# First convolution chunk from half projections: ten taps ahead, small moves at the start of a hybrid encoder layer

## The reference

```python
h = rms_norm(x, norm_mix_g)
proj = h @ w_in                       # 1024 x 3840
a_val, a_gate, u, g_conv, g_ssm = split(proj)      # 768, 768, 256, 1024, 1024 columns
# convolution branch
v = a_val * sigmoid(a_gate)           # 256 x 768
v = causal depthwise convolution of v, 31 taps, + conv_b
v = silu(layer_norm(v)) @ w_conv_out
# state-space branch: 16 groups, 64 complex states each
bu = u @ B_bar;  scan x_t = A x_(t-1) + bu_t;  y = Re(C x) + d * u;  gelu; glu; @ w_ssm_out
m = sigmoid(g_conv) * y_conv + sigmoid(g_ssm) * y_ssm
x = x + m @ w_out
# then x += MoE(rms_norm(x)): 32 experts, top 4 of each token, 12 MiB of weights an expert
# and a final rms_norm
```

## Time and profile before

| | |
|---|---|
| median of 3 runs | 1145.58 us |
| profiled execution, its time / its span | 1142.67 / 1140.9 us |
| chain of work that ended last | PE 89%, DVE 9% |
| PE busy | 1113.5 us, 98% |
| DVE busy | 273.7 us, 24% |
| ACT busy | 179.5 us, 16% |
| POOL busy | 75.9 us, 7% |
| DMA, 431.62 MB on the queue of SP | 91.2% of 16 engines' span |

### The profile page before, as it was taken

The page is one execution under the profiler, slowest core; times in us unless marked ns, Lnnn a source line. Parts: engine busy times, 40 slices in busy tenths (PEclk is TensorE's granted clock), DMA queues, the critical chain, the costliest instruction groups (busy, mean ns, idle before and its releaser), DMA issues.

```text
span 1140.9 us, 12748 instructions
## 1 busy us (share of the span) xinstructions
PE 1113.5 (98%) x4959; PEld 490.8 (43%) x4960; DVE 273.7 (24%) x661; ACT 179.5 (16%) x333; POOL 75.9 (7%) x155
## 2 busy tenths in 40 slices
PE   7999899899999999999999999999999999999997
PEld 6888685533333333333333333333333333333332
DVE  3999761311111111111111111111111111111112
ACT  3011221111111111111111111111111111111112
POOL 2975100000000000000000000000000000000000
PEclk9999899799999999999999999999999999999999
DMA  8843479489999999999999999999999999999994
GB/s 225 268 157 139 159 304 374 185 327 410 418 418 428 430 427 429 429 427 430 427 429 429 429 429 429 427 430 427 428 429 427 430 427 428 429 429 429 429 427 191
DMA packets 51618, 431.89 MB, mean 379 GB/s; under 512 B 6465, under 2 KB 22255, under 8 KB 25390
## 3 DMA queue, kind: packets, MB, share of 16 engines
q1 hardware_dynamic: 51598, 431.62, 91.2%
HBM read 430.56 MB, written 1.05 MB: 378 GB/s over the span
## 4 chain that ended last, share of the span: by engine, by line
PE 89%; DVE 9%; issue 1%; ACT 1%; DMA 0%; DVEq 0%; another core or an unknown queue 0%; SPq 0%; POOL 0%; POOLq 0%
PE bank L1286 39%; PE bank L1298 20%; PE bank L1306 10%; DVE bank L814 6%; PE bank L1259 5%; PE bank L1265 3%; PE bank L1221 2%; PE bank L1186 2%; PE bank L1078 2%; PE bank L1278 1%; DVE bank L835 1%; PE bank L1270 1%; PE bank L1174 1%; PE bank L1252 1%; DVE ring L843 0%
## 5 line engine op out<-in xcount | busy, mean ns | idle before, releaser
L1286 PE MATMUL bank<-ring,area 128*64 128x512 f32 x2048 | 451.7, 593 | 0.8 <-DMA ring<-w_gate_up 0.8
L1286 PEld LDWEIGHTS bank<-ring,area 128*64 128x64 f32 x2048 | 147.4, 137 | 281.8 <-issue 273.5
L1298 PE MATMUL bank<-ring,area 128*64 128x512 f32 x1024 | 226.8, 595 | 1.0
L969 DVE TENSOR_SCALAR area<-bank 128x512 f32<-128x512 f32 x32 | 22.1, 692 | 769.8 <-PE bank L1286 769.8
L1298 PEld LDWEIGHTS bank<-ring,area 128*64 128x64 f32 x1024 | 70.7, 137 | 136.6 <-issue 127.9
L1306 PE MATMUL bank<-area,spT 128*128 128x512 f32 x256 | 118.4, 605 | 0.0
L1078 PE MATMUL bank<-area,ring 128*128 128x256 f32 x480 | 109.4, 388 | 1.2 <-DVE area L751 1.2
L1078 PEld LDWEIGHTS bank<-area,ring 128*128 128x128 f32 x480 | 92.5, 195 | 16.8 <-DMA ring<-w_in 1.4
L660 ACT ACTIVATE area<-area 128x512 f32<-128x512 f32 x32 | 20.2, 630 | 497.7 <-DVE area L969 497.7
L1306 PEld LDWEIGHTS bank<-area,spT 128*128 128x128 f32 x256 | 46.0, 189 | 71.9 <-issue 71.9
L814 DVE SCALAR_TENSOR_TENSOR bank<-ring,spread,bank 128x256 f32<-128x256 f32 x174 | 69.0, 481 | 0.0
(11 more groups left out here) (241 smaller groups left out, 522.8 us busy)
## 6 DMA issues: line engine op xcount, KB each, us to landing
ring<-w_gate_up SPq DMA_DIRECT2D x120, 2048.0 KB, 30.3
ring<-w_down SPq DMA_DIRECT2D x60, 2048.0 KB, 28.7
ring<-w_gate_up SPq DMA_DIRECT2D x16, 1024.0 KB, 12.0
ring<-w_in SPq DMA_DIRECT2D x15, 1024.0 KB, 9.6
ring<-w_down SPq DMA_DIRECT2D x8, 1024.0 KB, 13.2
ring<-w_out SPq DMA_DIRECT2D x1, 4096.0 KB, 14.0
ring<-w_conv_out SPq DMA_DIRECT2D x1, 3072.0 KB, 12.7
rows<-x SPq DMA_DIRECT2D x2, 512.0 KB, 3.8
```

Source lines behind the costliest of these rows:

```text
L969: return v.tensor_scalar(gc, bank[4][:, :], 7.0, None, ALU.min)
L1286: last = mm(bank[4 + b][64 * h:64 * h + 64, :], heT[:, k % 4, k // 4 * 64:k // 4 * 64 + 64], w[:, b * FF + h * 512:b * FF + h * 512 + 512] ...
L1298: last = mm(bank[6][64 * h:64 * h + 64, :], actT[:, k % 4, k // 4 * 64:k // 4 * 64 + 64], w[:, k % 2, h * 512:h * 512 + 512], start=(k == ...
```

## The change

It has these parts.

- PE makes the first halves (m = 0) of the first two chunks, `a_gate` and `a_val` of channels 0 to 127, first; then the transposes of the taps' weights; then the two second halves. The halves lie in four banks (`half_bank`). New semaphores `half_pe` and `half_sig`.
- ACT takes the sigmoid of each half by itself. The copy of the taps' weights moves behind the two Sin and the first half's sigmoid.
- DVE multiplies each half by itself (`gated_half`), and runs the taps of block 0 alone until `LEAD = 10` are done. From there even blocks (lane 0) and odd blocks (lane 1) take turns, lane 0 being ten taps ahead. In the scan loop 8 instructions follow each scan, the last too. The wait for `raw_ready`, which protects the memory that the finished block 0 is written to, moves to the last tap of block 0.
- SP issues the second chunk of `w_in` directly behind the first, ahead of the taps' weights, and `ssm_b` ahead of `ssm_c`.
- ACT runs one Sqrt on constants before it waits for x.
- POOL's block of ones is made once, in `pick`, where `ones_1` was made; the later `ones` and its count in the wait at L1147 go. The product for the rank waits for 7 instead of 8.

```diff
-SCAN_TAPS = 4
+SCAN_TAPS = 8
+LEAD = 10
...
+        half_bank = [[bank[5][:, 0:T], bank[4][:, 0:T]], [bank[6][:, 0:T], bank[3][:, 0:T]]]
...
             load_win(0)
+            load_win(1)
             sp.dma_start(tap_rows, conv_w[0]).then_inc(tap_in, 16)
+            for ri, src in enumerate((ssm_b_re, ssm_b_im)):
+                sp.dma_start(ssb[:, ri, :, :], src[0].rearrange("(t g) p h -> (g p) t h", g=2)).then_inc(ssm_in, 16)
             for ri, src in enumerate((ssm_c_re, ssm_c_im)):
                 sp.dma_start(cld[:, ri, :, :], src[0].rearrange("(c g) h p -> (g h) c p", c=2)).then_inc(c_in, 16)
-            for ri, src in enumerate((ssm_b_re, ssm_b_im)):
-                sp.dma_start(ssb[:, ri, :, :], src[0].rearrange("(t g) p h -> (g p) t h", g=2)).then_inc(ssm_in, 16)
-
-            load_win(1)
...
-            g.memset(ones_1, 1.0).then_inc(ones_ready, 1)
+            g.memset(ones, 1.0).then_inc(ones_ready, 1)
...
-            g.memset(ones, 1.0).then_inc(consts, 1)
...
+            act.wait_ge(consts, 1)
+            s.activation(neg_top, ident[:, 0:2], ACT.Sqrt)
             for t in range(TT):
                 act.wait_ge(x_in[t], 16)
...
-            act.wait_ge(params_pe, 2)
-            s.activation(taps[:, :, :], bank[7][:, 64:64 + KC * W].rearrange("p (k w) -> p k w", w=W), ACT.Copy)\
-                .then_inc(params_sb, 1)
...
             s.activation(pw[:, 0, 0, :], ra, ACT.Sin).then_inc(act_sin, 1)
+            act.wait_ge(half_pe, 1)
+            s.activation(sig_a[:, 0, :], half_bank[0][0], ACT.Sigmoid).then_inc(half_sig, 1)
+            act.wait_ge(params_pe, 2)
+            s.activation(taps[:, :, :], bank[7][:, 64:64 + KC * W].rearrange("p (k w) -> p k w", w=W), ACT.Copy)\
+                .then_inc(params_sb, 1)
+            act.wait_ge(win_pe, 1)
+            s.activation(sig_a[:, 1, :], half_bank[0][1], ACT.Sigmoid).then_inc(win_act, 1)
...
+            def gated_half(m):
+
+                if m == 0:
+                    dve.wait_ge(half_pe, 2)
+                    dve.wait_ge(half_sig, 1)
+                else:
+                    dve.wait_ge(win_pe, 2)
+                    dve.wait_ge(win_act, 1)
+                ins = v.tensor_tensor(vT[:, m, W - 1:PADT], sig_a[:, m, :], half_bank[1][m], ALU.mult)
...
+            lanes = [[(k, w) for k in range(half, KC, 2) for w in range(W)] for half in range(2)]
+            order = lanes[0][:LEAD]
+            for n in range(KC // 2 * W):
+                order += lanes[0][LEAD + n:LEAD + n + 1] + lanes[1][n:n + 1]
...
+                for k, w in some:
+                    if w == 0 and k in (1, 2, 4):
+                        if k == 1:
+                            gated_half(1)
                         else:
...
+                            gated(k // 2)
+                    if (k, w) == (0, W - 1):
+                        dve.wait_ge(raw_ready, 1)
+                    tap(k, w)
...
-            gated(0)
-            dve.wait_ge(raw_ready, 1)
+            gated_half(0)
             dve.wait_ge(params_sb, 2)
-            taps_of(0, range(W))
-            gated(1)
-            taps_of(1, range(W))
-            gated(2)
+            scanning = len(order) - SCAN_TAPS * ST
+            taps_of(order[:scanning])
...
-                taps_of(2, range(SCAN_TAPS * t, SCAN_TAPS * (t + 1) if t < ST - 1 else W))
+                taps_of(order[scanning + SCAN_TAPS * t:scanning + SCAN_TAPS * (t + 1)])
...
-            project(0)
+            project(0, (0,))
+            project(1, (0,))
             pe.wait_ge(tap_in, 16)
...
-            project(1)
+            project(0, (1,))
+            project(1, (1,))
...
-            pe.wait_ge(consts, 7)
             pe.wait_ge(conv_done, KC)
```

More of the change, by code:

```diff
@@ L126, in build @@
         bdown = ring[0:E, 20 * CH:20 * CH + D]
[L127 removed]
+        tri = at(20, 128, 1024)
         rows = sb("rows", [128, TT, D])
@@ L147, in build @@
         pick = sb("pick", [128, TT, CAP])
+        ones = pick[:, :, :].rearrange("p t s -> p (t s)")
         spread = sb("spread", [128, TT, 2, CAP])
@@ L230, in build @@
         win_dve = sem("win_dve")
+        half_pe = sem("half_pe")
+        half_sig = sem("half_sig")
         bu_pe = sem("bu_pe")
@@ new lines, in _, with tap @@
+            last_tap = {}
+            def tap(k, w):
+                src, acc = vT[:, k, w:w + T], bank[2][:, k % 2 * T:k % 2 * T + T]
+                if w == 0:
+                    if k >= 2:
+                        dve.wait_ge(conv_done, k - 1)
+                    ins = v.tensor_scalar(acc, src, taps[:, k, 0:1], p_cb[:, k:k + 1], ALU.mult, ALU.add)
+                else:
+                    dve.wait_ge(dve_own, last_tap[k])
+                    ins = v.scalar_tensor_tensor(conv[:, k, :] if w == W - 1 else acc, src, taps[:, k, w:w + 1], acc,
+                                                 ALU.mult, ALU.add)
+                if w == W - 1:
+                    ins.then_inc(conv_done, 1)
+                else:
+                    own[0] += 1
+                    last_tap[k] = own[0]
+                    ins.then_inc(dve_own, 1)
@@ L1054, in _ @@
                 pe.wait_ge(diag_ready, t + 1)
-                last = mm(bank[6][:, t * 128:t * 128 + 128], ones_1, diag[:, t, :], start=True, stop=True)
+                last = mm(bank[6][:, t * 128:t * 128 + 128], ones, diag[:, t, :], start=True, stop=True)
             last.then_inc(spread_pe, 1)
@@ L1077, in project @@
                             pe.wait_ge(hT_ready, k + 1)
-                        last = mm(win_bank(n)[:, m * T:m * T + T], w[:, k, m * 128:m * 128 + 128], hT[:, k, :],
-                                  start=(k == 0), stop=(k == KD - 1))
+                        last = mm(half_bank[n][m] if n < 2 else win_bank(n)[:, m * T:m * T + T],
+                                  w[:, k, m * 128:m * 128 + 128], hT[:, k, :], start=(k == 0), stop=(k == KD - 1))
                 if 1 in ms:
                     last.then_inc(win_pe, 1)
+                elif n < 2:
+                    last.then_inc(half_pe, 1)
             def raw_transpose(raw, b):
```

27 lines of the change are left out of this document (8 added, 19 removed).

## The result

The changed kernel takes 1135.32 us in the median of 9 runs (1133.2 to 1140.17), the kernel before in the same comparison 1144.92 us (9 runs, 1142.28 to 1146.0). The profiled execution took 1134.46 us with a span of 1132.7 us; before 1142.67 and 1140.9. So the profiled executions differ by 8.2 us where the forecast had 6.4, and the medians by 9.6.

The account below looks back on a forecast made before the run. PE bounds nearly throughout, except DVE's convolution taps from about 30 to 130 us; PE and DMA are at their limit in the experts. 3.7 us (DVE) + 2.7 us (clock) = 6.4 us, giving 1139.2 us, range 1137.0 to 1142.8 us.

Parts of the forecast that it names:

- Sign, mechanism, and places: Faster: DVE's taps end earlier, PE's wait ahead of the channel sum shrinks, and the experts pass the gain on in full.
- The sum of DVE's terms: DVE up to the last tap: 0.55 + 4.3 - 1.15 = 3.7 us earlier, sum on PE at 127.0 us.
- The lone tap: DVE: a tap waiting for its predecessor costs 0.52 us, against 0.39 us when two lanes take turns.
- rival 2: DVE: lone taps cost nothing extra, gain 4.85 us there, total 1138.0 us; chance 0.05.
- The lead taps: DVE: first tap at 21.6 us; eleven lone taps fill the hole before the second half gate, taking 4.3 us off later.
- The clock behind the shorter wait: PE at the channel sum: clock stays at 2.4 GHz behind a 1.8 us wait, gaining 2.7 us; 3 chances in 4.
- Rival 1: PE at the channel sum: the clock falls again behind the 1.8 us wait, gain 3.7 us, 1141.9 us; chance 0.20.
- Transfers: Start: second w_in chunk lands by about 13.5 us, ssm_b by 18.5 at the latest; no gain of its own counted.
- If the rise comes at the same moment, 0.5 us more at half pace are 0.25 us of work at full pace: PE's first projections: starting 0.5 us earlier with an unchanged clock rise ends both chunks 0.25 us earlier.
- The later fall: PE clock, 211 to 228 us, ahead of the experts: fall stays, its shift worth up to 1.7 us either way.
- From profile to median: Whole kernel: the median lies 2.9 us above the profiled execution, and the same difference was kept for the changed kernel.
- Table load and block of ones: Start: early Sqrt saves a 1.28 us table load, 0.25 us taken; POOL's single block of ones worth nothing.

Follow-up runs that it names:

- e8: Kernel before, with filler products on PE around the last y_pair so it stays busy in its wait for the taps: 1140.19 us, ratio 0.9976.
- e3: Kernel before plus only the early Sqrt ahead of x: 1141.96 us, ratio 0.9988.
- e11: Changed kernel with 16 instead of 4 filler products in PE's later wait, at 197 us: 1131.54 us, ratio 0.9912 to the kernel before.
- pairs f: Four further profiled runs, two of each kernel unmodified, on one chip: 1145.48 and 1143.97 us before, 1132.64 and 1132.41 us changed.
- e7: Changed kernel with filler at PE's start and LEAD = 0, so no lead taps: 1135.18 us, ratio 0.993 to the kernel before.
- e4: Changed kernel with filler products at PE's start, forcing an early clock: 1132.73 us, ratio 0.9925 to the kernel before.
- e5: Kernel before with filler products at PE's start, forcing an early clock: 1145.59 us, ratio 1.0018.
- e6: Changed kernel with filler at PE's start and the old order of transfers: 1138.88 us, ratio 0.998 to the kernel before.
- f2: Changed kernel unmodified, a further profiled run paired with one of the kernel before: 1132.64 us.
- f1: Kernel before unmodified, a further profiled run paired with one of the changed kernel: 1145.48 us.
- f3: Kernel before unmodified, second further profiled run in the pairs: 1143.97 us.
- e9: Kernel before with only the changed kernel's order of transfers: 1145.15 us, ratio 1.001.
- e10: Kernel before with filler at PE's start and the new order of transfers: 1135.29 us, ratio 0.9934.
- e2: Changed kernel without the early Sqrt: 1134.30 us, ratio 0.9942 to the kernel before.
- e1: Changed kernel run again unmodified for a second trace: 1134.78 us, ratio 0.9945 to the kernel before.
- e12: Changed kernel with filler at PE's start and 16 instead of 4 products in its later wait: 1132.67 us, ratio 0.992 to the kernel before.

## Why the prediction was wrong, by its own steps

**Sign, mechanism, and places: right.** DVE's taps ahead of the sum set PE's wait; the wait shrank, the fall of the clock behind it went, and in this pair the experts kept their length (908.8 and 908.7 us) and so passed the gain on in full. Over all traces that stretch varies from 906.7 (e8) to 910.5 us (e3), longest where the fall reaches into it, so the passing on is known to a microsecond or two and no better. Where the clock came up as late as before (e11), first tap, hole, wait and sum come out within 0.3 us.

**The sum of DVE's terms: right at a like clock.** 3.7 us forecast, 3.8 in the pairs f. The lone tap: 0.52 us, as worked out; so rival 2 falls. The Trainium skill's page "VectorE: DVE Perf Modes", section "The DRAIN you can't avoid", found eight copies as fast with a semaphore behind each as with one behind the last. That holds one chain with semaphores against the same chain without, and no run here has lone taps without them; the 0.52 and 0.39 us here hold a dependent chain against two that take turns, all with semaphores. So the prediction's reading of that page, that lone taps would cost nothing extra, did not follow from it, and the trace does not contradict the page. The lead taps: the forecast's price for these ten is 3.9 (ten times 0.39) less 1.15 for the lone taps at the end, 2.75 us; the last tap moved by 2.2 us (e7 against e4). In e4 they end after PE is done, and the second half gate starts at 25.95 us where it starts at 25.36 without them, which is that difference of 0.6 us. The medians' 2.45 us holds the clock's two falls as well.

**The clock behind the shorter wait: right.** 2.7 us forecast, 2.6 in the profile (5.46 to 2.86), 2.7 by e8 with the taps as they were. Rival 1 (the clock falls again) did not come, but was near: 2.08 us idle in e7 were followed by a partial fall.

**Transfers: the times right, the price wrong.** The second chunk landed at 13.4 us (5.2 and 8.2 to landing; forecast 13.5), `ssm_b_im` at 17.5 (at the latest 18.5). But the move was priced at nothing, as cover for PE's new order. In the trace of before the large transfer is issued at 9.96 us behind the small ones, and PE came to it at 21.4 us only because its first chunk ran slowly. With that cover gone PE waits 1.95 us (e3), 4.41 (e5, with its later landing), 6.19 (e6). The move takes this bound away and is worth 6.2 us there (e6 against e4).

**The failed step: "If the rise comes at the same moment, 0.5 us more at half pace are 0.25 us of work at full pace".** It takes the moment of the rise in one execution for a property of the kernel. It is not one (7.14, 8.86 and 10.18 us for the first chunk in after, f2 and e11); the profiled execution of after had the early rise, and its first chunk took 7.14 instead of 9.93 us. Both chunks were done 3.5 us earlier (25.12 against 28.59 us), not 0.25. In the forecast's own terms, the 0.55 us by which the first tap behind the wait was to come earlier became 3.3 (26.13 against 29.42 us). So the sum came 6.5 us earlier where 3.7 were forecast, 2.8 us more. By e11, which differs from the changed kernel only behind the sum and had the late clock, 2.5 us of it are the clock's (126.71 - 124.21) and 0.3 the other sizes; the lead taps, which end after PE under the early clock, keep back the rest of its 3.0 us. I should have asked what an earlier rise does in either kernel: in the one before it stops at the transfer, in the changed one it goes through. (In the third course, with a smaller rise, the kernel before still gains: the sum at 129.22 us in f1, 1.5 us ahead of rows 1.) That asymmetry is a part of the change's effect on the median, in no term and in no rival.

**The later fall: in the profiled executions inside its bounds.** 1.7 us either way were allowed; the trace shows 1.1 us against the change. The pairs f, which had a longer fall before and a shorter one after, show 104.5 - 97.2 - 2.5 = 4.8 us for it, more than was allowed.

**From profile to median: the second failed step.** I carried the distance of 2.9 us between before's median and its profiled execution over to the changed kernel. Its own is 0.9 us. The distance wasn't a constant of measuring. Some of it was the median of only 3 runs: with 9 runs it is 1144.92, and the distance 2.25 us. For the rest the profiles offer a cause: the profiled execution of before had a short later fall (17 us where f1, f3, e3 and e9 have 27), and its start had not met the transfer as e3's did. How often either happens is not known, so this is argued and not shown.

**The account of the miss.** Forecast 1139.2, measured 1135.3, 3.9 us. In the profiled executions 2.8 us more gain up to the sum (2.5 of it the clock's at the start) and 1.1 us less from the later fall make 1.7 of the 1.8 us (8.2 - 6.4); the carried distance, 2.9 - 0.9, makes 2.0, of which 0.7 is the median of before that moved from 1145.58 to 1144.92. The first is shown: e4 and e5 force the early clock on both kernels, e6 and e10 give or take the order of the transfers, and e11 gives the changed kernel's sum under the late clock. That the early rise came in the profiled execution of after and not in that of before was luck, or has a cause that no run shows. The second is argued.

**Table load and block of ones: nothing**, as forecast for the ones; for the load 0.25 us were taken, and e2 shows no difference.

## What to carry to other kernels

A stretch at the lower clock can hide that a transfer is late: before pricing a move of transfers at nothing, work out when PE would come to the data if it ran at 2.4 GHz from the start, and hold that against the landing. Where a trace shows the clock rise inside a stretch, take the moment as one draw: price the change at both levels, and give each a chance. A distance between one profiled execution and the median can itself come from such differences, and should be in the range, not in the sum. And where profiles are to tell how often a course of the clock comes, take several of both kernels on one chip; here chip and course can't be told apart. A part of a change is best run alone, too: under a forced early clock the order of the transfers was worth 6.2 to 10.3 us (e6 against e4, e5 against e10), all the rest 2.6 to 6.7 (e10 against e4, e5 against e6).

## What the runs showed of the hardware that was not expected

The clock at the start has at least three courses, with a first chunk of 7.14 to 7.17, 8.83 to 8.86 or 9.4 to 10.2 us for the same 32 matmuls. The Trainium skill's page "TensorE: Matmul & The Clock Gate", section "Part 1: The HAM clock gate (the "warmup" mystery)", says as much, that the number of slow matmuls at the start differs by run, and calls the penalty under 1% of a kernel. The traces agree: 10.18 - 7.14 = 3.0 us are 0.3% of this kernel. But that is a third of the whole change, and what it does depends on which bound stands behind it.

The time from issue to landing of one and the same 1 MiB transfer was 9.9 us in e3 and 12.7 us in e5, with the same transfers ahead of it.

No rule by idle time alone holds here. Ahead of the sum, and at the second chunk, falls stood behind 1.95 us (e3) and, in part, 2.08 us (e7), none behind 1.78 (e6), 1.77 (e11), 1.76 (f2) and 1.13 (after). But at the first projection 1.15 us idle was followed by a fall in f1 and f3 and by none in e3; and the same place in the later stage, with 3.31 us idle in after and in e1, was followed by about 20 and 17 us at half, in f2 by about 14. With 0.67 us idle there in e11 and e12 there still were about 7 and 11.
